# Mixers of a two-layer decoder kernel: a matrix of ones made on the chip, B's rows loaded whole, u projected by halves, W_out's second half loaded first, and v centred on ScalarE at other places

## The reference

```python
hn = rmsnorm(x, norm_mix[layer]); z = hn @ w_in[layer]           # 1024 -> 3 * 512
ua, ub, vb = z[..., :512], z[..., 512:1024], z[..., 1024:]
# group A, S5: per channel group, 64 complex states
s[t] = a * s[t-1] + (q * B) @ ua[t];  y = Re(C @ s) + D * ua      # a, q from a_re, a_im, log_dt
ya = glu(gelu(y))
# group B, spatial gating, 8 heads of 64
v = layernorm(gelu(vb));  yb = gelu(ub) * (tril(W_s) @ v + b_s)
x = x + concat(rmsnorm(ya), rmsnorm(yb)) @ w_out[layer]
x = x + (swiglu(rmsnorm(x)) if layer == 0 else moe_top2_of_8(rmsnorm(x)))
```

## Time and profile before

| | us |
|---|---|
| median of 3 runs | 994.45 (990.79 to 995.15) |
| the profiled execution | 997.04 |
| its span in the trace | 995.2 |
| PE busy | 941.5 (95%) |
| DVE busy | 705.6 (71%) |
| ACT busy | 522.7 (53%) |
| POOL busy | 323.6 (33%) |
| chain that ended last, by engine | PE 79%, DVE 10%, DMA 5%, issue 3%, ACT 2% |

### The profile page before, as it was taken

How to read it: one execution, slowest core, us unless ns; L and a number is a source line. 1 busy time by engine, 2 the same in 40 slices (tenths; PEclk the granted TensorE clock), 3 DMA queues, 4 the chain that set the end, 5 groups by cost and what they waited for, 6 DMA issues and landing times.

```text
span 995.2 us, 15155 instructions
## 1 busy us (share of the span) xinstructions
PE 941.5 (95%) x5526; PEld 790.5 (79%) x5526; DVE 705.6 (71%) x1032; ACT 522.7 (53%) x679; POOL 323.6 (33%) x259
## 2 busy tenths in 40 slices
PE   6999999999999999799998999999999999999995
PEld 5476779999999996486786888878788788878774
DVE  7799557573455328965655496979798977988884
ACT  3661445453344214641623566766676857676762
POOL 7996002212446102930110052141405151323311
PEclk9999999999999999899996899999999999999998
DMA  9500735555544219005400688898888988898971
GB/s 271 161 1 7 299 88 187 164 160 150 166 140 154 74 24 300 1 4 198 205 1 29 244 295 314 290 370 280 300 299 310 345 286 304 283 376 282 385 228 48
DMA packets 95564, 199.65 MB, mean 201 GB/s; under 512 B 34194, under 2 KB 55922, under 8 KB 95508
## 3 DMA queue, kind: packets, MB, share of 16 engines
q1 hardware_dynamic: 94708, 197.88, 58.9%
q10 hardware_dynamic: 576, 0.59, 0.2%
q0 software_dynamic: 224, 0.43, 0.1%
HBM read 197.27 MB, written 1.61 MB: 200 GB/s over the span
## 4 chain that ended last, share of the span: by engine, by line
PE 79%; DVE 10%; DMA 5%; issue 3%; ACT 2%; SPq 0%; DVEq 0%; ACTq 0%
PE ps L1288 7%; PE ps L1287 7%; PE ps L1290 7%; PE ps L1025 6%; PE ps L1026 6%; PE ps L1027 6%; PE ps L1199 5%; PE ps L1358 4%; PE ps L1359 3%; PE ps L1362 3%; DMA wraw_u<-in_moe_w_gate 3%; PE ps L1038 3%; PE ps L1020 2%; PE ps L1190 2%; DVE M L1406 2%
## 5 line engine op out<-in xcount | busy, mean ns | idle before, releaser
L779 ACT ACTIVATE wrnd_g<-wraw_g 128x1376 fp32r<-128x1376 f32 (+2 forms) x96 | 115.4, 1213 | 64.8 <-DMA wraw_g<-in_moe_w_down 32.7
L647 POOL TENSOR_TENSOR wrnd_g<-wraw_g,wrnd_g 128x1024 fp32r<-128x1024 f32 (+2 forms) x16 | 48.8, 3049 | 297.1 <-ACT wrnd_g L779 297.1
L1406 DVE TENSOR_TENSOR wrnd_u<-wraw_u,wrnd_u 128x1376 fp32r<-128x1376 f32 (+1 forms) x80 | 135.2, 1719 | 3.4 <-ACT wrnd_u L779 2.9
L1406 DVE TENSOR_TENSOR wrnd_g<-wraw_g,wrnd_g 128x1376 fp32r<-128x1376 f32 (+1 forms) x80 | 121.9, 1536 | 19.7 <-ACT wrnd_g L779 19.5
L779 ACT ACTIVATE wrnd_u<-wraw_u 128x1376 fp32r<-128x1376 f32 (+1 forms) x96 | 115.5, 1256 | 12.8 <-DMA wraw_u<-in_moe_w_gate 8.1
L647 POOL TENSOR_TENSOR wrnd_u<-wraw_u,wrnd_u 128x1376 fp32r<-128x1376 f32 (+1 forms) x16 | 54.4, 3401 | 84.1 <-ACT wrnd_u L779 84.1
L1025 PE MATMUL ps<-Md,split_u 128*128 128x288 f32 (+2 forms) x240 | 71.7, 299 | 5.4 <-DVE rs L1406 5.4
L1406 DVE TENSOR_TENSOR xb<-xb,ps 128x288 f32<-128x288 f32 x96 | 39.6, 447 | 49.1 <-PE ps L1199 25.6
L1027 PE MATMUL ps<-Md,split_u 128*128 128x288 f32 (+2 forms) x240 | 70.9, 296 | 0.0
L1025 PE MATMUL ps<-Md,split_d 128*128 128x288 f32 (+2 forms) x224 | 66.0, 295 | 0.8 <-DVE xb L1406 0.8
L1027 PE MATMUL ps<-Md,split_d 128*128 128x288 f32 (+2 forms) x224 | 65.6, 293 | 0.0
(11 more groups left out here) (354 smaller groups left out, 2671.7 us busy)
## 6 DMA issues: line engine op xcount, KB each, us to landing
wraw_u<-in_moe_w_gate SPq DMA_DIRECT2D x39, 688.0 KB, 6.3
wraw_g<-in_moe_w_up SPq DMA_DIRECT2D x32, 688.0 KB, 7.1
wraw_g<-in_moe_w_down SPq DMA_DIRECT2D x39, 512.0 KB, 4.5
wraw_u<-in_moe_w_down SPq DMA_DIRECT2D x33, 512.0 KB, 4.4
wraw_u<-in_moe_w_up SPq DMA_DIRECT2D x24, 688.0 KB, 5.8
wraw_g<-in_moe_w_gate SPq DMA_DIRECT2D x18, 688.0 KB, 5.9
raw<-in_ffn_w_gate SPq DMA_DIRECT2D x20, 512.0 KB, 4.6
raw<-in_ffn_w_up SPq DMA_DIRECT2D x20, 512.0 KB, 3.8
```

The source lines that it names most:

```text
L647: pool.tensor_tensor(lo[0:r, 0:w], raw_half(n)[0:r, 0:w], hi[0:r, 0:w].bitcast(F32), ALU.subtract).then_inc(w_lo_pool, 1)
L779: act.activation(halves(n)[0][0:r, 0:w], raw_half(n)[0:r, 0:w], ACT.Copy).then_inc(w_hi, 1)
L1406: return dve.tensor_tensor(o, a, b, op)
```

## The change

It has seven parts.

1. `ones` is no part of the loaded `consts` any more: DVE sets it by a memset, PE then runs 18 matmuls of `ones` by `ones` into a bank that nobody reads (`WARM_START`), and `consts` and `misc` are loaded behind W_in's second piece. PE waits for them behind v.
2. B is loaded once for both parts, in rows of 4 KB, into `b_raw` (the place of `ct1` and `ct2`, which POOL uses later: it waits for `b_used`), and no longer into `BPX` in runs of 128 bytes. W_in's first piece goes ahead of it in layer 0.
3. In layer 0, h is made by ACT, ahead of the squares, and not by DVE. PE does `u_half(0)` ahead of the mean's matmuls, as it did in layer 1 already.
4. `load_out` waits for the chunk states' matmuls, loads pieces 2 and 3, then waits for `st_ready` and loads 0 and 1.
5. v's tile 0 is centred by ACT (`centre(0)`), where `centre(1)` stood; `centre(1)` stands behind the copies of B and of the states, ahead of `centre(2)`.
6. DVE takes the reciprocal of v's deviation and `nmr` (minus mean over deviation), now for 16 heads, ahead of `carried` in layer 1.
7. `layer_norm(1)` and the last tile's `nmr` (`last_rows`) move into DVE's first round of rotation and scan.

PE, start of the program, before: L1020 is the mean, L1038 ua, L1052 the transposes of 1/rms, L1060 v.

```diff
...
 OUT_AFTER = ((0, 0, 0, 0, 0, 0, 2, 3), (0, 0, 0, 0, 1, 4, 5, 6))
+
+WARM_START = 18
 SCATTER_BANK = (3, 4, 5, 6, 7, 6, 7, 6)
...
                 for r in range(2)]
+        b_raw = D[:, 5248:6272].rearrange("p (r n f) -> p r n f", r=2, n=NP)
         ct1 = D[:, 5248:5760].rearrange("p (n f) -> p n f", n=NP)
...
                 sp.dma_start(x[:, 4 * j:4 * j + 4, :], x_d[:, 4 * j:4 * j + 4, :]).then_inc(x_in[j], 16)
-            sp.dma_start(consts[:, :], consts_d).then_inc(const_in, 16)
-            sp.dma_start(misc[:, :], misc_d).then_inc(const_in, 16)
...
                     sp.wait_ge(rot_ready, 2)
-                for r in range(2):
-                    sp.dma_start(BPX[:, r, :, 0, :], b_d[l, :, r]).then_inc(prep_in, 16)
+                else:
+                    piece(0, 0, 4, 0)
+                sp.dma_start(b_raw, b_d[l]).then_inc(prep_in, 16)
+                piece(1, 4, KT, 0)
                 if l == 0:
-                    piece(0, 0, 4, 0)
-                piece(1, 4, KT, 0)
+                    sp.dma_start(consts[:, 0:4 * P], consts_d[:, 0:4 * P]).then_inc(const_in, 16)
+                    sp.dma_start(misc[:, :], misc_d).then_inc(const_in, 16)
                 for r in range(2):
...
                 src = w_out_d[l].rearrange("(k p) f -> p k f", p=P)
-                for j in range(PIECES):
+                for j in (2, 3, 0, 1):
+                    if j == 0:
+                        sp.wait_ge(st_ready, 2 * (l + 1))
                     sp.dma_start(w_out[:, 2 * j:2 * j + 2, :], src[:, 2 * j:2 * j + 2, :]).then_inc(w_out_in[j], 16)
...
                 sp.wait_ge(rot_ready, l + 1)
-                sp.wait_ge(st_ready, 2 * (l + 1))
+                sp.wait_ge(s_mm, 4 * (l + 1))
                 load_out(l)
...
                 pool.wait_ge(c_in, 32 * (l + 1))
+                pool.wait_ge(b_used, l + 1)
                 link(pool.tensor_scalar(CPX[:, 1, :, 0, :], CPX[:, 1, :, 0, :], -1.0, None, ALU.mult))
...
                 def centre(t):
-                    act.wait_ge(nmr_ready, 2 * l + t)
+                    n = TILES[t][1]
+                    act.wait_ge(nmr_ready, 2 * l + (2 if t == 2 else 1))
                     for g in range(NH):
-                        vh, at = v[:, t, g * HD:(g + 1) * HD], t * NH + g
-                        vc = act.activation(vh, vh, ACT.Identity, bias=nmr[:, at:at + 1], scale=std[:, at:at + 1])
+                        vh, at = v[0:n, t, g * HD:(g + 1) * HD], t * NH + g
+                        vc = act.activation(vh, vh, ACT.Identity, bias=nmr[0:n, at:at + 1], scale=std[0:n, at:at + 1])
                     vc.then_inc(vc_ready, 1)
...
                 if l == 0:
+                    for k in range(KT):
+                        act.wait_ge(x_in[k // 4], 16)
+                        act.activation(h[:, k, :], x[:, k, :], ACT.Copy, scale=col(0, "norm_mix", k)).then_inc(h_ready, 1)
                     squares(x, sq0[0], 0, lambda k: act.wait_ge(x_in[k // 4], 16))
...
                 deviation(0, 16, 1)
-                centre(1)
+                centre(0)
                 gelu_v(2)
...
                     ss.then_inc(s_ready, 1)
+                centre(1)
                 centre(2)
...
-            pe.wait_ge(const_in, 32)
+            pe.wait_ge(ones_ready, 1)
+            for n in range(WARM_START):
+                pe.matmul(bank(6, P), ones, ones, start=True, stop=True)
             for l in range(DEPTH):
...
-                if l == 0:
-                    mean_sum(sq0[0], 0, KT, 7, 0)
                 u_half(0)
...
                     pe.wait_ge(xadd, X_DENSE[1] + 8)
-                    mean_sum(sq0[1], 0, KT, 7, 24)
+                mean_sum(sq0[l], 0, KT, 7, 24 * l)
                 u_half(4)
...
+                pe.wait_ge(const_in, 32)
                 pe.wait_ge(bp_ready, l + 1)
...
+            dve.memset(ones, 1.0).then_inc(ones_ready, 1)
             link(dve.memset(eps[:, :], EPS))
...
                         angle_dve(0, part, sv)
-                    for k in range(KT):
-                        dve.wait_ge(x_in[k // 4], 16)
-                        gained(h[:, k, :], 0, "norm_mix", k)
                 else:
...
-                dve.wait_ge(prep_in, 32 * (l + 1))
+                dve.wait_ge(prep_in, 16 * (l + 1))
                 for s in range(CH):
                     fr, fi = (bc(sv(26), 32), bc(sv(28), 32)) if s == 0 else (bc(sv(10), 32), bc(sv(11), 32))
-                    br, bi = BPX[:, 0, :, max(s - 1, 0), :], BPX[:, 1, :, max(s - 1, 0), :]
+                    br, bi = [BPX[:, r, :, s - 1, :] if s else b_raw[:, r] for r in range(2)]
                     o_r, o_i = BPX[:, 0, :, s, :], BPX[:, 1, :, s, :]
...
                     link(tt(o_i, fr, bi, ALU.mult))
-                    tt(o_r, o_r, bt1, ALU.subtract)
+                    o_r = tt(o_r, o_r, bt1, ALU.subtract)
+                    if s == 0:
+                        o_r.then_inc(b_used, 1)
                     last = tt(o_i, o_i, bt2, ALU.add)
...
-                    n, g = TILES[t][1], slice(8 * t, 8 * t + 8)
-                    vt = v[0:n, t, :].rearrange("p (h d) -> p h d", h=NH)
-                    if t:
-                        dve.wait_ge(vc_ready, 2 * l + t)
-                    else:
-                        link(tt(vt, vt, bc(stat[0:n, g, 0], HD), ALU.subtract))
-                        link(tt(vt, vt, bc(std[0:n, g], HD), ALU.mult))
+                    n = TILES[t][1]
+                    dve.wait_ge(vc_ready, 3 * l + t + 1)
                     link(tt(v[0:n, t, :], v[0:n, t, :], lng[0:n, :], ALU.mult))
...
                 statistics(1).then_inc(var_ready, 1)
+                dve.wait_ge(std_ready, 2 * l + 1)
+                link(dve.reciprocal(std[:, 0:16], std[:, 0:16]))
+                dve.scalar_tensor_tensor(nmr[:, 0:2 * NH], stat[:, 0:2 * NH, 0], -1.0, std[:, 0:2 * NH],
+                                         ALU.mult, ALU.mult).then_inc(nmr_ready, 1)
                 if l:
                     carried()
-                dve.wait_ge(std_ready, 2 * l + 1)
-                link(dve.reciprocal(std[:, 0:16], std[:, 0:16]))
-                dve.scalar_tensor_tensor(nmr[:, NH:2 * NH], stat[:, NH:2 * NH, 0], -1.0, std[:, NH:2 * NH],
-                                         ALU.mult, ALU.mult).then_inc(nmr_ready, 1)
                 layer_norm(0)
                 statistics(2).then_inc(var_ready, 1)
-                layer_norm(1)
-                dve.wait_ge(std_ready, 2 * l + 2)
-                link(dve.reciprocal(std[:, 16:24], std[:, 16:24]))
-                dve.scalar_tensor_tensor(nmr[:, 2 * NH:3 * NH], stat[:, 2 * NH:3 * NH, 0], -1.0, std[:, 2 * NH:3 * NH],
-                                         ALU.mult, ALU.mult).then_inc(nmr_ready, 1)
+
+                def last_rows():
+
+                    dve.wait_ge(std_ready, 2 * l + 2)
+                    link(dve.reciprocal(std[:, 16:24], std[:, 16:24]))
+                    dve.scalar_tensor_tensor(nmr[:, 2 * NH:3 * NH], stat[:, 2 * NH:3 * NH, 0], -1.0,
+                                             std[:, 2 * NH:3 * NH], ALU.mult, ALU.mult).then_inc(nmr_ready, 1)
...
                     link(tt(wr, wr, tmp, ALU.add))
+                    if q == 0:
+                        last_rows()
                     tt(v8(wi), si, cr, ALU.mult)
...
                     if q == 0:
+                        layer_norm(1)
                         layer_norm(2)
...
```

More of the change, by code:

```diff
@@ L354, in build @@
         const_in = sem("const_in")
+        ones_ready = sem("ones_ready")
+        b_used = sem("b_used")
         prep_in = sem("prep_in")
```

## The result

The changed kernel takes 1000.57 us in the median (995.66 to 1004.42), the kernel before 994.89 beside it: ratio 1.0057, 95% interval 1.0033 to 1.008. It is slower by a little, where 986.8, 7.7 us less, was forecast. Every ratio in this document leaves out runs that lie more than 1.5% above the fastest of their kernel. The profiled execution took 1001.56, its span is 999.7 (before 995.2).

| | before | after | difference | forecast |
|---|---|---|---|---|
| v, layer 0 | 30.97 | 40.03 | +9.1 | +2.8 |
| ub, layer 0 | 63.97 | 75.26 | +11.3 | +4.0 |
| GLU, layer 0 | 105.53 | 118.66 | +13.1 | +3.2 |
| first ua, layer 1 | 368.19 | 377.76 | +9.6 | -0.4 |
| 24 transposes, layer 1 | 418.34 | 426.03 | +7.7 | -5.3 |

What follows compares the result with a forecast made beforehand. PE, busy 95% of the span, was taken as the bound, so only its stalls and slow stretches could be won. Layer 1 -7.3, layer 0 to the readout +3.2 and W_out -3.6 sum to -7.7: 994.45 to 986.8 us, range 980.5 to 993.5.

Steps and rivals of the forecast that it cites:

- Layer 0, the start: Layer 0 up to the readout: the late root of the mean starts v 2.8 us later; +3.2 us (+1 to +6).
- rival B: Layer 0 loses more: v at the lower clock (+2.4) and `layer_norm(1)` exposed beside POOL (+1 to 2.8); 990.8, chance 0.24.
- Layer 1, reciprocal ahead of `carried`: Layer 1, ahead of the 24 transposes: earlier reciprocal cuts PE's wait by 5.4 us, the kept clock gives 2.4 more.
- I take off 0.5 us for DVE's powers of B: Layer 1: POOL starts a little earlier beside DVE's powers of B, a loss of 0.5 us.
- Layer 1, what is late next: Layer 1, DVE's first round with `last_rows` and `layer_norm(1)`: hidden behind PE's ub projection, with 3 us to spare.
- Layer 0, W_out: Layer 0, output matmuls: earlier loads of pieces 2 and 3 end two waits and the slow clock; -3.6 us (-1.5 to -3.6).
- a shift goes through whole: Both FFNs behind the mixers load from the mixers' end, so time won or lost there reaches the end in full.
- E: Layer 0: v runs at the lower clock for most of its length, +14 us; 1000.8, chance 0.05.
- D: Layer 1 gains only 3 to 5: clock stays down, or PE waits for DVE's `vn_ready`; 990.5 to 992, chance 0.08.

## Why the prediction was wrong

The forecast was 7.7 us less and the span grew by 4.5, so it missed by 12.2. By the first table 6.3 of this had come by layer 0's v, 13.0 by layer 1's transposes and 15.5 by its ub; 3.1 came back between there and the GLU by no term of the forecast (before, PE stood 2.41 us there, see below). That part is luck.

**The step that failed first is *Layer 0, the start*.** Its price for s = 1 and 2 behind the late root was 9.8 us (9.1 to 10.6). It measured 13.2, and 11.0 in the run with POOL's wait, where the clock stayed up and the stretch began 2.1 us earlier. I had reasoned that POOL would be ahead, and bounded the stretch by the row of before; but the stretch as a whole was shifted, and DVE's operations met POOL's long ones at other places (the row of 1.74 us, where the earlier trace rows have 1.42). The other part is the root: ready at 24.1 and not 21.5. The landing of W_in was 1.0 late (10.01), and ua's first half cost 1.8 more at the lower clock after 3.04 us of standing, a stand that I had put at nothing ("PE stood until the constants landed at 7.7"). The sum, 2.7 + 3.4 + 0.1, is the 6.2 us from 33.8 to 40.03. Moving the root's wait takes the queue's part away (5.8 us at the same clock), more ones take away the clock's. Then v itself: PE stood 8 us, resumed at 0.50, and v to ub took 35.2 us and not 33.0, so +2.2. That is rival B's mechanism (+2.4), which I had kept out of the forecast. The Trainium skill (TensorE: Matmul & The Clock Gate, Part 1: The HAM clock gate) lets the clock fall with PE's recent idleness; the fall in the window 10 to 12, behind 3.04 us of standing, and the 0.50 at 36 us, within the stand of 8.01, agree with it. The three stands of 1.68 to 2.70 us cost no clock.

**The second is *Layer 1, reciprocal ahead of `carried`*.** The wait behind `carried` went as forecast (0.03 us behind the root). The term that was mis-sized stands in the next part, "I take off 0.5 us for DVE's powers of B": it is 3.0 us. With B in long rows POOL, whose idle time the profile puts down to the load of the running states in both kernels, starts 2.1 us earlier against v, and more of DVE's operations lie beside it. Then `nmr` was 1.17 us and not 0.78, so 1.9 us came of 5.4 less 0.5. PE still stood 5.25 us, so the 2.4 us of the clock did not come at all. Delaying POOL restored both. The long rows alone, in the kernel before, moved it the same way (2.0 of the 3.0 us, and PE stood 1.4 us longer); what the other 1.0 is, no run shows. The Trainium skill (GPSIMD Engine Reference, 1. Specifications) says that GpSimd and VectorE share an SBUF interface; I had weighed it for `layer_norm(1)` and not for the powers of B, where it told.

***Layer 1, what is late next*.** Of the two layer norms in the first round nothing came onto the path in the changed kernel. But this was luck of the late start: with v early in layer 0, the two layer norms cost 2.3 to 2.8 us and the clock behind them. And I had looked for the next wait in the scan only. With the reciprocal alone moved, the next wait is the variance of v's last tile, behind `layer_norm(0)`. The change's fifth part takes two of its four operations off DVE. In the run with POOL's wait, which has that part, the chunk states to ub take 8.0 us, where they took 14.0 with the reciprocal alone; that this is the fifth part's doing is not shown.

***Layer 0, W_out*: right.** -3.6 was forecast, -3.7 measured from the GLU to the FFN, in the changed kernel and alone. In the time of the whole kernel no run could tell it from nothing.

**Missing from the forecast: what a gain is worth behind it.** I wrote that a shift goes through whole. Through the FFNs it did (9.4 us at layer 0's FFN and 9.6 at layer 1's ua; 4.7 at layer 1's GLU and 4.5 at the end), inside a mixer it did not. In layer 0's mixer before, the gating stretch runs at 1.00 and ub to GLU takes 41.6 us. In the six kernels without filler in which PE came to it over 1 us earlier, it ran at 0.73 to 0.90, and ub to GLU took 46.1 to 54.2. That is one reason why single repairs recovered 6 to 8 us but two together came to 990.3 and not 986.8. Another is that single gains share a part: in the run with POOL's wait the clock ahead of ua stayed up too. Which weighs more, no run shows. Why some executions keep the clock there and others not stays open. So does the 1.86 us that PE stood ahead of the row at 117.59 for no releaser that the profile shows; before had such a stall of 2.41 us at 470.56, in layer 1, and not there. The prediction supposed that such stalls move with the program's addresses, which no run shows. In both places loads filled the DMA engines (share 1.03 to 1.09), but with 30 matmuls of ones they did too (1.03 at 110 to 112), and the stall was not there.

By rivals: of B's two mechanisms one was at work, v at the lower clock, at its price (2.2 for 2.4); the other, `layer_norm(1)` exposed, was not, and v's start at 40.03 and not 33.8 is outside B as well. E named the time (1000.8) by a mechanism that did not happen, v at the lower clock for 12 us and more: the clock was back 6 us after v's start. That it hit is luck. No rival had slower by a late start of v plus the loss in layer 1. D's own time was off as well: a gain of 3 to 5 in place of 7.3 gives 989.1 to 991.1, not 990.5 to 992.
